# Re-spacing side work among the ten units of the attention ring: weight splits, selection rounds, a mask and a set of transposes

## The reference

```
h = rms_norm(x, ln1_g);  parts = split(h @ w_in)
a_out = dsa_mixer(...)   # 4 heads; per query only the 64 keys with the highest index score take part
b_out = s5_mixer(...)    # complex diagonal state space; y = gelu(y); y = y * sigmoid(y @ glu_w + glu_b)
c_out = nsa_mixer(...)   # 8 heads; compressed, selected and window branches, gated
x = x + concat(rms_norm(a_out), rms_norm(b_out), rms_norm(c_out)) @ w_out
x = x + square(relu(rms_norm(x) @ w_up)) @ w_down
```

## Time and profile before

| what | value |
|---|---|
| time, median of 3 | 640.77 us (640.45 to 640.81) |
| the profiled execution, its own time | 640.45 us |
| its span | 638.7 us |
| mean granted TensorE clock | 0.998 |
| PE busy | 615.2 us (96%) |
| DVE, ACT, POOL busy | 419.6, 359.8, 240.6 us |
| chain that ended last | PE 78%, DVE 7%, POOL 7%, ACT 5% |

### The profile page before, as it was taken

How to read it: one execution, slowest core, us unless ns; L and a number is a source line. 1 busy time by engine, 2 the same in 40 slices (tenths; PEclk the granted TensorE clock), 3 DMA queues, 4 the chain that set the end, 5 groups by cost and what they waited for, 6 DMA issues and landing times.

```text
span 638.7 us, 11293 instructions
## 1 busy us (share of the span) xinstructions
PE 615.2 (96%) x4298; PEld 532.7 (83%) x4298; DVE 419.6 (66%) x766; ACT 359.8 (56%) x652; POOL 240.6 (38%) x417
## 2 busy tenths in 40 slices
PE   7989989999999999999999999999999999999995
PEld 6867866789999899889888787668999899889984
DVE  7699896396655795874576877638755554554563
ACT  5755689646546535453475658983654453454451
POOL 5899678405226999900004207870000000000001
PEclk9999999999999999999999999999999999999999
DMA  9674704255875457366638540414476656656631
GB/s 262 212 194 134 152 8 112 63 177 167 262 227 175 159 175 238 116 230 201 193 94 284 110 125 3 117 34 138 154 246 189 192 171 201 195 172 195 193 101 66
DMA packets 55440, 102.79 MB, mean 161 GB/s; under 512 B 12713, under 2 KB 18906, under 8 KB 55354
## 3 DMA queue, kind: packets, MB, share of 16 engines
q1 hardware_dynamic: 48986, 96.04, 49.3%
q0 software_dynamic: 1792, 4.07, 2.8%
q10 hardware_dynamic: 4608, 1.97, 1.2%
HBM read 99.69 MB, written 1.31 MB: 158 GB/s over the span
## 4 chain that ended last, share of the span: by engine, by line
PE 78%; DVE 7%; POOL 7%; ACT 5%; issue 2%; DMA 1%; SPq 0%; POOLq 0%; DVEq 0%; ACTq 0%
PE pb L1777 75%; DVE w_lo L1354 2%; ACT tab_zone L1154 2%; POOL dtmp L826 1%; POOL sp L607 1%; DVE sc_zone L1670 1%; PE pb L1931 1%; PE pb L1803 1%; DMA proj<-in_ln_g 1%; POOL yz L607 1%; ACT ptmp L1168 1%; PE pb L2197 1%; POOL w_lo L787 1%; ACT w_hi L908 1%; POOL sp L612 1%
## 5 line engine op out<-in xcount | busy, mean ns | idle before, releaser
L1354 DVE TENSOR_TENSOR w_lo<-raw,w_hi 128x1024 fp32r<-128x1024 f32 (+2 forms) x176 | 223.4, 1286 | 128.6 <-ACT w_hi L908 127.6
L908 ACT ACTIVATE w_hi<-raw 128x1024 fp32r<-128x1024 f32 (+2 forms) x184 | 187.4, 1027 | 186.1 <-PE pb L1777 170.1
L1777 PE MATMUL pb<-h_hi,w_hi 128*128 128x256 f32 x512 | 145.4, 284 | 0.6 <-DVE w_lo L1354 0.5
L1777 PE MATMUL pb<-h_hi,w_lo 128*128 128x256 f32 x512 | 144.9, 283 | 0.0
L1777 PE MATMUL pb<-h_lo,w_hi 128*128 128x256 f32 x512 | 144.8, 283 | 0.0
L1777 PE MATMUL pb<-w_hi,z_hi 128*128 128x512 f32 x256 | 100.0, 391 | 0.4 <-DVE w_lo L1354 0.4
L1777 PEld LDWEIGHTS pb<-h_hi,w_hi 128*128 128x128 f32 x512 | 98.2, 192 | 2.4 <-issue 1.3
L1777 PE MATMUL pb<-w_hi,z_lo 128*128 128x512 f32 x256 | 99.8, 390 | 0.0
L1777 PE MATMUL pb<-w_lo,z_hi 128*128 128x512 f32 x256 | 99.6, 389 | 0.0
L1777 PEld LDWEIGHTS pb<-h_hi,w_lo 128*128 128x128 f32 x512 | 98.2, 192 | 0.4
L1777 PEld LDWEIGHTS pb<-h_lo,w_hi 128*128 128x128 f32 x512 | 98.2, 192 | 0.0
(11 more groups left out here) (314 smaller groups left out, 885.7 us busy)
## 6 DMA issues: line engine op xcount, KB each, us to landing
raw<-in_w_up SPq DMA_DIRECT2D x64, 512.0 KB, 4.0
raw<-in_w_down SPq DMA_DIRECT2D x64, 512.0 KB, 4.1
raw<-in_w_in SPq DMA_DIRECT2D x24, 512.0 KB, 4.9
raw<-in_w_out SPq DMA_DIRECT2D x8, 512.0 KB, 4.7
raw<-in_w_out SPq DMA_DIRECT2D x16, 256.0 KB, 5.4
raw<-in_w_in SPq DMA_DIRECT2D x8, 308.0 KB, 3.6
raw<-in_w_in SPq DMA_DIRECT2D x8, 280.0 KB, 2.9
x<-in_x ACTq DMA_DIRECT2D x4, 256.0 KB, 4.5
```

The costliest lines, as they stand in the source:

```text
L908: hi_made.by(act.activation(w_hi[:, n % RING, 0:width(n)], raw[:, n % RING, 0:width(n)], ACT.Copy))
L1354: lo_made.by(dve.tensor_tensor(w_lo[:, n % RING, 0:width(n)], raw[:, n % RING, 0:width(n)], w_hi[:, n % RING, 0:width(n)].bitcast(F32), AL ...
L1777: return pe.matmul(o, l, r, start=start, stop=stop, skip_group_check=True)
```

## The change

Five things move and one operation is replaced:

- ACT converts piece 22 ahead of the tanh at unit 3 (before: behind it) and piece 23 behind the copy at unit 5 (before: ahead of the copy at unit 6).
- POOL splits piece 23 behind unit 5 (before: unit 7).
- In layer 1 POOL makes group A's mask behind unit 5 (before: unit 2). In layer 0 it is behind unit 5 as before, with the split now ahead of it.
- In layer 0 DVE's rounds go from units 0, 1, 2, 2, 3, 4, 5, 6 to 0, 1, 2, 3, 4, 5, 6, 6.
- PE transposes group B's rows at the end of unit 6's work, ahead of the scores of unit 7 (before: right behind these scores).
- POOL's scaling in units 8 and 9 is a `tensor_scalar` with a column as its scalar (before: a `tensor_tensor` with the column broadcast).

```diff
--- before.py
+++ after.py
@@ -417,7 +417,7 @@
 
         pairs = [("C", br, b) for br in range(2) for b in range(4)] + [("A", 0, b) for b in range(2)]
         C_PAIRS = C_HEADS
-        LO_OUT = (None, 1, 3, 7)
+        HI_OUT = (None, 1, 3, 5)
 
         def load_b(eng, lyr, s):
 
@@ -820,20 +820,19 @@
                     for m in range(2):
                         i = 2 * (p % 2) + m
                         for t, (a, z) in enumerate(((0, PART), (PART, 384))):
+                            pool.nop(nofuse=True)
                             if kind == "C":
-                                pool.nop(nofuse=True)
                                 col = 12 * m + 3 * b + 1 + br
                                 w = pool.tensor_scalar(pn[:, i, a:z], ex[:, i, a:z], cf[:, i, t:t + 1],
                                                        gate[:, t, col:col + 1], ALU.mult, ALU.mult)
                             else:
-                                w = pool.tensor_tensor(pn[:, i, a:z], ex[:, i, a:z],
-                                                       cf[:, i, t:t + 1].to_broadcast([PART, z - a]), ALU.mult)
+                                w = pool.tensor_scalar(pn[:, i, a:z], ex[:, i, a:z], cf[:, i, t:t + 1], None, ALU.mult)
                             if (m, t) != (1, 1):
                                 step(w, False)
                     pn_sb.by(w)
-                    if p in LO_OUT:
-                        lo_out(20 + LO_OUT.index(p))
-                    if p == (5 if L == 0 else 2):
+                    if p in HI_OUT:
+                        lo_out(20 + HI_OUT.index(p))
+                    if p == 5:
                         pool.wait_ge(topped.sem, topped.at(L, 1))
                         pool.nop(nofuse=True)
                         a_flag.by(pool.tensor_scalar(abias, isc, -2e38, NEG, ALU.is_gt, ALU.mult))
@@ -1156,8 +1155,6 @@
                                 if (m, t) != (1, 1):
                                     step(w, False)
                         e_sb.by(w)
-                    if p == 6:
-                        hi(L, 23)
                     if p >= 2:
                         v = p - 2
                         act.wait_ge(pT_ps.sem, pT_ps.at(L, v + 1))
@@ -1178,15 +1175,14 @@
                         cq_turned(1)
                     if p == 4 and L < DEPTH - 1:
                         c_table(L + 1, 6)
-                    if p == 1:
-                        hi(L, 21)
+                    if p in HI_OUT:
+                        hi(L, 20 + HI_OUT.index(p))
                     if p == 2:
                         act.wait_ge(y_ps.sem, y_ps.at(L, 1))
                         y_sq.by(act.activation(yt, pb[7][:], ACT.Square, scale=0.044715 ** 0.5))
                     if p == 3:
                         act.wait_ge(y_in.sem, y_in.at(L, 1))
                         y_th.by(act.activation(y2, y2, ACT.Tanh, scale=GELU_A))
-                        hi(L, 22)
                     if p == 5:
                         act.wait_ge(cs_max.sem, cs_max.at(L, 1))
                         cs_exp.by(act.activation(pc2[:], pc2[:], ACT.Exp))
@@ -1650,7 +1646,7 @@
                            6: [], 7: [], 8: [], 9: [], 10: [], 11: []}
                 for p, work in ((3, y_cube), (4, y_gelu), (5, c_max), (6 + D, c_probs), (9, y_glu)):
                     between[p].append(work)
-                for p in ((0, 1, 2, 2, 3, 4, 5, 6) if L == 0 else (0, 0, 2)):
+                for p in ((0, 1, 2, 3, 4, 5, 6, 6) if L == 0 else (0, 0, 2)):
                     between[p].append(top)
                 assert 8 * sum(works.count(top) for works in (*behind.values(), *between.values())) == TOPK
                 last_slot = max(p for p, works in between.items() if top in works)
@@ -2161,7 +2157,7 @@
                 if L == 0:
                     between[4].append(next_c)
                 D = int(L == 0)
-                for p, work in ((7 + D, c_transpose), (9 + D, c_values), (1, s5_near), (2, s5_far), (8, glu)):
+                for p, work in ((7 + D, c_transpose), (9 + D, c_values), (1, s5_near), (2, s5_far), (6, y_turned), (8, glu)):
                     between[p].append(work)
                 for p in range(UNITS + 4):
                     if p < UNITS:
@@ -2182,8 +2178,6 @@
                                 d = slice(HD * m, HD * m + HD)
                                 w = mm(pb[m][:, a:a + n], q[d, t * PART:(t + 1) * PART], k[d, 0:n], t == 0, True)
                         s_ps.by(w)
-                    if p == 7:
-                        y_turned()
                     if 3 <= p < UNITS + 3:
                         v = p - 3
                         pe.wait_ge(pn_sb.sem, pn_sb.at(L, v + 1))
```

## The result

The changed kernel takes 645.94 us (median of 6, 645.24 to 647.98), the kernel before 640.79 on the same chip (median of 6, 640.45 to 641.37). The ratio is 1.0083, with a 95% interval of 1.0068 to 1.0098: 5.15 us slower, where 642.0 was forecast and 643.1 was the end of the range.

What follows compares the result with a forecast made beforehand. TensorE has no slack behind either layer's attention stretch, so delays there move the kernel's end. Plus 1.5 us (layer 0) and minus 0.2 (layer 1) on 640.45 gave 641.75, written 642.0 against the median; range 640.5 to 643.1.

Steps and rivals of the forecast that it cites:

- Step 1: Layer 0, DVE: a selection round moves from behind unit 2 to behind unit 6; DVE gains 0.2 us at most.
- step 2: Layer 0: ACT converts piece 22 before the tanh, 0.5 us later GELU; unit 5 stays put, within 0.2 us.
- Step 3: Layer 0: two selection rounds behind unit 6 delay unit 7's masked copy and unit 8's scores; PE's path 1.0 us late.
- step 4: Layer 0, POOL: piece 23's split ahead of the mask delays scaling 6 to 107.0; copy of unit 6 1.6 us late.
- Step 5: Transposes of the GELU's rows before unit 7's scores fall into PE's 1.25 us wait; counted as nothing, 0.5 us if uncovered.
- Step 6: Units 8 and 9, POOL: scaling by a column instead of a broadcast tensor makes no difference, within 0.3 us either way.
- The term of layer 1: Layer 1's attention: mask and split both behind unit 5; worth minus 0.2 us, between minus 0.3 and plus 0.15.
- PE's part: Layer 1: later masked copy of unit 7 makes PE 0.15 us late, or up to 0.5 early if the division shrinks.
- my second rival: Layer 1: moved transposes wait for late loads; up to 1.6 us there, total 643.9, or 642.9 landing at 409.0; chance 0.12.
- the third rival: Layer 1 wins nothing, DVE being as slow beside the split as beside the scalings: plus 1.5 to 1.65, 642.3; chance 0.12.
- One sign that the prediction named for layer 1: Layer 1: no POOL wait before unit 6's exponentials; the companion sign was a wait over 1 us before unit 8's.
- The first rival: Layer 1: POOL's wait was the whole trouble; layer 1 wins 1.4 us, total 640.9, if scaling 6 ends by 414.4; chance 0.16.

Runs made afterwards that it cites:

- after_again: The changed kernel once more, nothing altered: 646.99 us against 641.61 for the kernel before, ratio 1.008.
- a_twocol: Changed kernel with the scalings of units 8 and 9 also multiplied by a second column, of ones: 644.85 us against 641.84 for the kernel before.
- a_mended: Changed kernel with broadcast scalings in units 8 and 9 and ACT's compressed exponential ahead of piece 23's conversion: 645.06 us against 641.61 for the kernel before.
- a_noscale: Changed kernel with the scalings of units 8 and 9 back in broadcast form: 645.82 us against 642.36 for the kernel before.
- a_expfirst: Changed kernel with ACT's exponential of the compressed scores ahead of the conversion of piece 23: 644.37 us against 642.36 for the kernel before.
- a_noturn: Changed kernel with the transposes of the GELU's rows back behind the scores of unit 7: 646.86 us against 642.36 for the kernel before.
- b_flag: Kernel before with only layer 1's mask moved from unit 2 to unit 5: 640.80 us against 641.84 for the kernel before.
- a_lo7: Changed kernel with POOL's split of piece 23 back behind unit 7: 645.48 us against 641.84 for the kernel before.
- after: The changed kernel itself as first measured, with all parts of the change: 645.94 us against 640.79 for the kernel before.

## Why the prediction was wrong, by its own steps

The direction and the place were right; the time was not. The forecast's sum was +1.5 and -0.2; the stretches measured +2.08 and +2.67. That is 4.75 of the 5.9 us between the two profiled executions, and 1.07 more lie ahead of unit 5, 0.29 of them the change's. Together 5.04, where the medians are 5.15 us apart.

Step 1 and step 2 (the round behind unit 2, the tanh behind the conversion) were to cancel within 0.2 us. Unit 5 comes 0.29 us late as counted from unit 2, just past that bound; so it does in after_again and in six of the seven variants of the changed kernel, at 0.30 to 0.32; only a_twocol has none of it (11.60 us). Step 3, alone, cost 1.21 us (1.0 forecast), and lay beside step 4 in the whole. Step 4 is right step by step: with the entry taken off, scaling 6 is at 106.96 (107.0 forecast), the exponentials of unit 8 at 109.01 (109.04), the copy of unit 6 at 110.78 (110.8). Layer 0 without the new form is at +1.58 and +1.53 in two kernels, where 1.5 was taken; with what lies ahead of unit 5 it is 1.88 and 1.83, past the 1.7 at which its bounds ended. Step 5 (the transposes) was right for layer 0 and on the kernel before, and wrong inside the change, as below.

**Step 6 failed.** It took the column form for as long as the nearest rows, which had two multiplications, with 0.3 us either way, "ACT's own work hides either". The group measured 3.0 us and not 1.96, outside my bounds, and it wasn't hidden: PE waits 0.98 and 1.08 us for it. It costs 0.50 and 0.65 us in the changed kernel, 3.45 us on the kernel before. The step's reference row was of another form than the operation added; a_twocol, which has the reference row's form, measured what the step took (446 and 552 ns).

**The term of layer 1 failed**, -0.2 against +2.0 without the form. POOL's part of it was right: with layer 0's 3.18 us taken off, scaling 5 is at 406.83 (406.8 forecast) and scaling 6 at 413.86 (413.6). PE's part was wrong. It had unit 7's masked copy 0.95 us late "less what the division may win"; it came 2.29 us late, for either of two reasons:

- The wait for the loads, my second rival. Its place and its point were right: the loads are issued 1.0 us later against layer 0's shift (406.11 less 3.18 is 402.93, from 401.93), because the tanh stands behind the conversion, and the last landed at 411.66 less 3.18, 408.48, past the 408.1 up to which a wait was covered. Its price was too low: it put layer 1 at +0.6 us for a landing at 409.0, which makes 642.9, and here a landing at 408.48 went with +2.0 (a_mended and a_noscale, without the slow form). PE comes out of the wait at half its clock: the scores of unit 7 take 0.72 us more, and the transposes behind them 1.49 where they took 0.87. Neither the forecast nor the rival had a term for that. (The rival's own worst case, 643.9, lay past the 643.1 at which the range ends.)
- The division beside the split, the mechanism of the third rival, by which layer 1 would merely win nothing. I sized it by the row of DVE's instruction, 0.64 us. What goes with the wait is the length of POOL's instruction: 0.54 us beside scalings of 0.45 to 0.56 us each, 2.05 us beside a split of 2.36. The SBUF — State Buffer page of the Trainium skill (section Terms) says that VectorE and GpSimd arbitrate for a shared port pair by a lock that is "exclusive, held for the full instruction"; the trace agrees, in that the 16 elements ended 0.03 us after the split. It goes the other way too: where the 256-element multiplication came first (a_expfirst, a_mended) the split took 2.53 and 2.52 us, and not 2.36.

Where one of the two was undone and the other stayed, nothing was won: a_noturn is the slower for it, and a_mended's layer 1 is that of a_noscale (38.36 and 38.40).

One sign that the prediction named for layer 1 came, the other didn't. ACT's exponentials of unit 6 don't wait for POOL any more. Those of unit 8 don't either, where a wait of over 1 us was written: scaling 6 had ended at 419.00, and ACT reached them at 420.00 without idle time, late from its 2.38 us wait for PE. So POOL's path, by which the term of layer 1 was sized, was not the one that ended last. The first rival, that POOL's wait was the whole trouble in layer 1, was right for the mask by itself: b_flag has 1.24 us of the 1.4 it named. Its condition, scaling 6 through by 414.4, failed only because the split was put in the same place.

What stays open: the loads to `ytok` release PE either 4.3 us after the start of their issue (a_expfirst, a_lo7, a_twocol) or 5.6 (after, after_again, a_noscale, a_mended, a_noturn), from kernels with the same order of loads up to there. The slowest of the four landed 2.3 us after its issue in the first group and 3.5 to 3.6 in the second. No run varied only that, and what makes it slow isn't shown. That half of the clock follows PE's idle time is what the slices show in all six profiles of held kernels; it wasn't tried by itself, and how much of each hold is the wait and how much the clock isn't separated.

## What to carry to other kernels

When side work is moved on a queue, write down what the other engines do in the same microsecond, and not only what stands in the queue: a 2.4 us instruction of GpSimd can hold a tiny one of VectorE until it ends. A load that is issued later and wanted earlier needs its latest landing, not its median, in the sum, and a TensorE wait of 2 us is priced with the slow matmuls behind it. Of a bundle of moves try each alone on the old kernel: here one line, the mask of layer 1, was worth 1.24 us of its stretch, the transposes nothing, and the rest cost. Then try them in pairs: in layer 1 the moved mask alone gained and the moved split alone cost nothing, and in the kernels with both the split fell on the division.

## What the runs showed of the hardware

- GpSimd's multiplication by one column, without a second operation, took 650 and 924 ns for 128 and 256 elements per partition (615 and 934 in the changed kernel). With a second column it took 446 and 552, and the two-tensor form with a broadcast 406 and 618. Per further element that is 2.1, 0.8 and 1.7 ns. The GPSIMD Engine Reference of the Trainium skill (section 3.1, Elementwise — side-by-side cycle accounting) puts bodies of up to two operations at 1.03 cycles an element and the two-input form at about 2.6. By it an element would cost either column form 0.4 of what it costs the two-input form. The trace has 0.5 for two columns and 1.3 for one: the form with one operation is the slowest.
- TensorE was granted down to 0.50 of its clock, the 1.2 GHz level, in slices of 2 us behind single waits of 1.93 to 1.96 us (0.50 in after, 0.57 in a_mended) and behind three shorter ones in a row (0.64, 1.33 and 0.67 us in a_twocol; 0.98, 1.05 and 0.67 in a_noturn). Eight score matmuls then took 1.65 us and not 0.93. Behind waits of 0.65 and 0.31 us (a_lo7) or 0.60 and 0.79 (before) it kept 1.00. No run tried this alone.
- A VectorE multiplication of 16 elements took 2.04 to 2.06 us beside a GpSimd subtraction of 2.36 us, and 0.18 to 0.54 us in the kernels where the two didn't meet.
- Layer 1's stretch repeats to 0.1 us in the two kernels that were profiled twice (35.15 and 35.08; 39.05 and 39.01), while the whole varies by a few us. Such distances can tell kernels apart where the interval of the whole can't.
